# Order of a group's four projections: keys, first queries, values, second queries

## What is computed

```python
proj = x @ w_in                                   # queries, and keys/values of three branches
q_rot = apply_rope(q, cos, sin)                   # rotary position on queries
k_slc = apply_rope(kv_heads(ks), cos, sin);  v_slc = kv_heads(vs)
k_win = apply_rope(kv_heads(kw), cos, sin);  v_win = kv_heads(vw)
s_c = einsum(qn, k_cmp) * scale                   # compressed branch, unrotated queries
s_s = einsum(qr, k_sel) * scale;  s_w = einsum(qr, k_band) * scale
out = g0 * softmax(s_c) @ v_cmp + g1 * softmax(s_s) @ v_sel + g2 * softmax(s_w) @ v_band
```

## Time and profile before

| | us |
|---|---|
| median of 3 runs | 1373.08 (1370.35 to 1373.63) |
| the profiled execution | 1374.31 |
| its span, first to last instruction | 1372.5 |
| scores of the first unit start at | 91.44 |
| last product of the last group starts at | 330.07 |

### The profile page before, as it was taken

The page is one execution under the profiler, slowest core; times in us unless marked ns, Lnnn a source line. Parts: engine busy times, 40 slices in busy tenths (PEclk is TensorE's granted clock), DMA queues, the critical chain, the costliest instruction groups (busy, mean ns, idle before and its releaser), DMA issues.

```text
span 1372.5 us, 19855 instructions
## 1 busy us (share of the span) xinstructions
PE 1322.0 (96%) x6858; PEld 1108.3 (81%) x6858; DVE 635.4 (46%) x1469; ACT 674.6 (49%) x1257; POOL 599.4 (44%) x399
## 2 busy tenths in 40 slices
PE   8979999979999999999999999998999999999997
PEld 6868887867898888888888788887898888888885
DVE  3347777775544433440006767768354343341005
ACT  4347777765444444442214767776354444443122
POOL 2267767763434444444444222222244444444441
PEclk9999999999999999999999999999999999999999
DMA  9442322222323333334333321322424333334321
GB/s 296 108 102 61 85 70 78 69 70 97 99 82 108 92 95 103 92 105 131 101 92 95 87 62 49 94 64 62 154 78 123 92 92 98 100 93 137 103 66 62
DMA packets 172798, 131.98 MB, mean 96 GB/s; under 512 B 24544, under 2 KB 156244, under 8 KB 172724
## 3 DMA queue, kind: packets, MB, share of 16 engines
q1 hardware_dynamic: 172724, 131.02, 33.0%
HBM read 117.17 MB, written 4.39 MB: 89 GB/s over the span
## 4 chain that ended last, share of the span: by engine, by line
PE 82%; DVE 5%; issue 4%; ACT 4%; POOL 2%; DMA 2%; SPq 1%; DVEq 0%; POOLq 0%; ACTq 0%
PE ps L964 15%; PE ps L965 15%; PE ps L966 15%; PE ps L1218 7%; PE ps L1221 7%; PE ps L1219 7%; PE ps L1124 3%; PE ps L1138 2%; PE ps L1091 2%; PE ps L1264 2%; PE ps L1260 2%; PE ps L1259 2%; DVE ptl L1507 1%; DVE prob L1489 1%; PE ps L1137 1%
## 5 line engine op out<-in xcount | busy, mean ns | idle before, releaser
L488 POOL TENSOR_TENSOR wl<-raw,wh 128x1024 fp32r<-128x1024 f32 x178 | 426.3, 2398 | 648.0 <-ACT wh L611 647.9
L964 PE MATMUL ps<-xh,wh 128*128 128x512 f32 x968 | 381.8, 394 | 4.2 <-ACT work L900 3.9
L965 PE MATMUL ps<-xl,wh 128*128 128x512 f32 x968 | 377.9, 390 | 0.0
L966 PE MATMUL ps<-xh,wl 128*128 128x512 f32 x968 | 377.4, 390 | 0.0
L611 ACT ACTIVATE wh<-raw 128x1024 fp32r<-128x1024 f32 x192 | 201.2, 1050 | 191.8 <-PE ps L1221 182.2
L964 PEld LDWEIGHTS ps<-xh,wh 128*128 128x128 f32 x968 | 182.2, 188 | 41.9 <-ACT work L900 5.8
L966 PEld LDWEIGHTS ps<-xh,wl 128*128 128x128 f32 x968 | 181.9, 188 | 38.8
L965 PEld LDWEIGHTS ps<-xl,wh 128*128 128x128 f32 x968 | 182.1, 188 | 33.4
L1664 DVE SCALAR_TENSOR_TENSOR work<-ps,conv,work 128x511 f32<-128x511 f32 x88 | 66.0, 750 | 222.0 <-ACT work L847 156.7
L705 ACT ACTIVATE prob<-prob,negmax 128x128 f32<-128x128 f32 x192 | 107.4, 559 | 69.4 <-DVE negmax L1489 67.5
L1218 PE MATMUL ps<-wh,gh 128*128 128x512 f32 x352 | 137.1, 390 | 0.0
(11 more groups left out here) (197 smaller groups left out, 1948.8 us busy)
## 6 DMA issues: line engine op xcount, KB each, us to landing
raw<-in_ffn_w_up SPq DMA_DIRECT2D x88, 512.0 KB, 3.8
raw<-in_ffn_w_down SPq DMA_DIRECT2D x44, 512.0 KB, 3.6
raw<-in_fox_w_in SPq DMA_DIRECT2D x24, 512.0 KB, 4.0
raw<-in_nsa_w_in SPq DMA_DIRECT2D x12, 512.0 KB, 4.9
xt<-in_x SPq DMA_DIRECT2D x8, 512.0 KB, 5.0
raw<-in_nsa_w_in SPq DMA_DIRECT2D x16, 256.0 KB, 3.8
qs<-work SPq DMA_DIRECT2D x32, 128.0 KB, 2.3
raw<-in_nsa_w_o SPq DMA_DIRECT2D x8, 512.0 KB, 4.1
```

Source lines behind the costliest of these rows:

```text
L488: nc.gpsimd.tensor_tensor(wl[:, slot, :, :], raw[:, slot, :, :], wh[:, slot, :, :].bitcast(F32), ALU.subtract).then_inc(s_wl, 1)
L964: nc.tensor.matmul(o, ah, bh, start=start, stop=False)
L965: nc.tensor.matmul(o, ah, bl, start=False, stop=False)
L966: return nc.tensor.matmul(o, al, bh, start=False, stop=stop)
```

## The change

The order of a group's items becomes keys, queries 0, values, queries 1 (`KIND`). The queries 1 of group g are no longer projected before the group starts but in its own first six steps (`NSA_STEPS`): two ksteps in each of steps 0 and 1, then one in each of steps 2 to 29; steps 30 and 31 have none. So group 0's queries 1 leave the prologue, and the last group has eight ksteps in its steps 0 to 5. `NSA_EARLY` starts in step 8 instead of 2. The work on an item stands two steps earlier in its pass of eight steps (copy in step 5 instead of 7, sine product in 7 instead of 1). The values are transposed in step 30 instead of 19.

```diff
+KIND = (0, 2, 1, 3)
-NSA_EARLY = {2: (0, 0), 6: (1, 0), 12: (2, 0), 18: (3, 0), 21: (0, 1), 24: (1, 1), 27: (2, 1), 30: (3, 1)}
+NSA_EARLY = {8: (0, 0), 11: (1, 0), 14: (2, 0), 17: (3, 0), 20: (0, 1), 23: (1, 1), 26: (2, 1), 29: (3, 1)}
+NSA_STEPS = [(0, 2), (2, 4)] + [(v + 2, min(v + 3, 32)) for v in range(2, 32)]
@@ SP
-            for n in range(6, NSA_ITEMS):
-                item_moves(n - 6)
+            load_item(6)
+            item_moves(1)
+            for n in range(7, NSA_ITEMS):
+                if n > 8:
+                    item_moves(n - 7)
                 load_item(n)
@@ POOL, prologue
-            for n in range(3):
-                if n != 1:
-                    rope_cos(0, n)
-                    rope_sum(0, n)
-                    for h in range(1 if n else 2):
-                        rope_lo(0, n, h)
-                lo(n + 7, (n + 7) % R)
+            for n in range(2):
+                rope_cos(0, n)
+                rope_sum(0, n)
+                for h in range(1 if n else 2):
+                    rope_lo(0, n, h)
+            for c in range(7, 10):
+                lo(c, c % R)
@@ POOL, in the groups
-                    if turned and w == 0:
-                        rope_cos(*item)
-                    if turned and w == 2:
-                        rope_sum(*item)
+                    if 3 < n <= NSA_ITEMS and before[1] != 2:
+                        if w == 0:
+                            rope_sum(*before)
+                    if n < NSA_ITEMS and n % 4 != 2 and w == 6:
+                        rope_cos(*divmod(n, 4))
@@ ACT, in the groups
-                    if g < GROUPS - 1 and w == 7:
-                        item_copy(g + 1, v // 8)
+                    if n < NSA_ITEMS and w == 5:
+                        item_copy(*divmod(n, 4))
@@ DVE, in the groups
-                    if turned and w == (6 if item[1] == 1 else 1):
-                        item_dve(*item)
+                    if n < NSA_ITEMS and n % 4 != 2 and w == 7:
+                        item_dve(*divmod(n, 4))
+                    if v == 0 and g:
+                        item_dve(g, 2)
@@ PE, in the groups
-                    if g < GROUPS - 1:
-                        n = 4 * (g + 1) + v // 8
-                        if v % 8 == 0:
-                            pe.wait_ge(s_pf, n)
-                        kstep(4 + n, (4 + n) % R, v % 8)
+                    for s in range(*NSA_STEPS[v]):
+                        n = 4 * g + 3 + s // KB
+                        if n < NSA_ITEMS:
+                            if s % KB == 0:
+                                pe.wait_ge(s_pf, n)
+                            kstep(4 + n, (4 + n) % R, s % KB)
-                    if v == 19 and g < GROUPS - 1:
-                        pe.wait_ge(s_cl, u // 16 + 1)
-                        values_turn(g + 1)
+                    if v == 30 and g < GROUPS - 1:
+                        pe.wait_ge(s_cmask, u // 16 + 2)
+                        values_turn(g + 1, BX)
```

More of the change, by code:

```diff
@@ L405, in load_out @@
                 for k in range(KB):
[L406 to L408 removed]
+                    if c0 == C_WO0 and k < 7:
+                        item_moves(NSA_ITEMS - 7 + k)
+                    if c0 == C_WO0 and k == 7:
                         move_queries(NSA_ITEMS - 1)
@@ L598, in _ @@
             for g in range(GROUPS):
-                for n in range(2):
+                for n in (0, 2):
                     RAW_EXTRA[(4 + 4 * g + n) % R] += 1
             def landed(c):
-                return sum(2 if 4 <= x < C_WO0 and (x - 4) % 4 < 2 else 1 for x in range(c + 1) if x % R == c % R)
+                return sum(2 if 4 <= x < C_WO0 and x % 2 == 0 else 1 for x in range(c + 1) if x % R == c % R)
             def hi(c, slot, n=None):
@@ L752, in _ @@
                     u, w = 32 * g + v, v % 8
-                    item = (g, 3) if v < 8 else (g + 1, v // 8 - 1)
-                    turned = v < 8 or g < GROUPS - 1
+                    n = u // 8 + 3
                     for x in ([0, 1, 2] if u == 0 else [v + 2]):
@@ L776, in _ @@
                         heads_hi(u // 16 - 1, oh)
[L777 to L781, removed]
+                    if 3 < n <= NSA_ITEMS and n % 4 != 3 and w == (n % 4 == 1):
+                        item_hi(*divmod(n - 1, 4))
+                    if v == 31 and g < GROUPS - 1:
+                        item_hi(g + 1, 2)
+                    if u // 8 < NSA_ITEMS - 2 and w == 2:
+                        hi(u // 8 + 10, (u // 8 + 10) % R)
             head_copy(HEADS - 1, 4 * HEADS, BO + 1)
@@ L1113, in cmp_turn @@
                 pe.wait_ge(s_cp, j + 1)
+                if j % 2 == 0 and j:
+                    pe.wait_ge(s_pl, 2 * j + 3)
                 for i in range(QT):
@@ L1164, in first_tile @@
                 down_half(c0 + k, k, 0, h, oh, ol, OUT_AT, k == 0, False)
+            pe.wait_ge(s_kc, 3)
+            item_steps(0)
+            conv_turn(0)
+            item_steps(1)
+            cmp_hidden(1)
+            pe.wait_ge(s_kc, 4)
+            item_steps(2)
+            pe.wait_ge(s_gel, 2)
+            for g in range(GROUPS):
+                for hb in range(2):
+                    last = nc.tensor.matmul(ps[0:NCMP, 4, g * HD:(g + 1) * HD], ghid[:, hb, g * NCMP:(g + 1) * NCMP], w2v[:, hb, :],
+                                            start=(hb == 0), stop=(hb == 1))
+            last.then_inc(s_cmpo, 1)
             pe.wait_ge(s_cmpr, 1)
             cmp_scores(0)
-            item_steps(3)
+            values_turn(0, BO)
+            conv_turn(1)
             pe.wait_ge(s_vc, 4)
@@ L1571, in _ @@
             conv_copy(1)
-            for step in (cmp_mask, cmp_difference, cmp_sum, cmp_inverse, cmp_gate, cmp_scale):
+            for step in (cmp_sum, cmp_inverse, cmp_gate, cmp_scale):
                 step(0)
```

119 lines of the change are left out of this document (52 added, 67 removed).

## The result

| | kernel before | changed kernel |
|---|---|---|
| median (lowest to highest), us | 1373.10 (1370.35 to 1373.63) | 1382.55 (1381.74 to 1383.22) |
| span of the profiled execution, us | 1372.5 | 1381.0 |
| mean granted clock | 0.994 | 0.988 |

The ratio is 1.0069, with a 95% interval of 1.0053 to 1.0085: **slower by 9.4 us**, where the prediction said 6.7 us faster. The prediction was wrong in its sign, and 1382.55 lies outside its range. (One execution of a later run, at a mean granted clock of 0.842, took 1492.48 us; it is among the ten of that run's median, 1377.22, and is left out of its ratio.)

The account below looks back on a forecast made before the run. PE was taken to bound groups 0 to 2, the chain over DVE, ACT and POOL the last. Prologue -6.3, groups -0.9, last group 0, less 0.5 for lateness: -6.7, 1366.4 us; range 1362.5 to 1371.5.

Parts of the forecast that it names:

- Its first step: Groups 0 to 2: PE, busy 56.8 of 59 us in a filled group, was taken to set the pace.
- Part 1: Prologue: one item leaves and queries 0 come first, so unit 0's maximum comes 6.3 us earlier (bounds 5 and 7.5).
- the rule on the rings: Prologue: rings work in issue order, so scores would wait for two weight loads, some 1 us later than 84.7.
- Part 2: Groups 0 to 2: PE's 58 us each stay; -1.9 us gained and 1.0 us of crowding added, net -0.9 us.
- The gain at the group starts: Starts of groups 1 to 3: PE's waits of 0.6 us for the queries' transfer fall away, -1.9 us.
- The term for crowding: Groups 0 to 2: moved work on ACT, POOL and DVE costs 1.0 us over three groups, bounds 0 and 4.
- Part 3: Last group: the moved item's 5.5 us of PE come back; net taken as 0, range -1.3 to +2.4 us.
- the case I had given -1.3: Last group: swap takes 4 us, DVE waits some 1.5 us, second block takes 14.5 us; -1.3 us, weighed 2 to 1.
- the 0: Last group: net change taken from short and long swap landings weighed 2 to 1, range -1.3 to +2.4 us.
- B: Groups 0 to 2: ACT's backlog in steps 17 and 18 reaches PE, 4 us per group, +6.2, 1379.3 us; chance 0.08.

## Why the prediction was wrong

**Its first step.** "So groups 0 to 2 go at PE's pace" was read from 96% busy and from 56.76 busy of 59.00. The kernel before without swaps shows PE's pace: 171.4 us for units 0 to 96. Before stood 8.0 us above it. The chain over four engines paid part of each wait already (12.8 us of waits, 8.0 us of time), so there was no free cover to lay new waits under. PE's list of waits showed it, in nine short ones that come to 6.2 us: besides the two lines of rows 6 it has this one.

```profile
PE ps L1138 <- DVE ptl L1507: 2.4, 4, 0.8
```

No line of it is long, and I had looked for long ones.

**Part 1** held. -5.7 against -6.3: scores at 85.5 where I had 84.3 to 84.7. The miss lies in the moves: the scores came 3.3 us after the issue of the last one was over, not 2.2:

```profile
79.64 1.33 SPq L365 DMA_DIRECT2D qs<-work  x2
81.02 1.23 SPq L368 DMA_DIRECT2D qs<-work  x2
```

That is the 1 us of the rule on the rings that I had weighed and not taken (the Trainium skill, DMA: Bandwidth & Descriptors, Queues, rings and completion order); the trace agrees with it in size, and in the run with the moves ahead of the loads the last two landed 2.4 us after they were issued, where they took 3.6 here. DVE was done with its list at 85.4, as the 85.6 had it, but then waited 0.83 us for those scores, so its maximum was at 86.23. PE waited 6.0 us, where I had 4.8.

**Part 2** is the failure: +13.4 for -0.9. The gain at the group starts was real, PE's list has no wait there any more. The term for crowding, 1.0 with bounds of 0 and 4, was mis-sized by 14: with the gain of 1.9 it came to 15.3, 5.1 us a group. Even its own bound did not add up, since 0.8 us at two places per group is 4.8 and not 4. It rested on "the nearest row is POOL's wait, 0.8 us per group", which priced a crowd in the order of before and not one more in a place that has no slack. Without swaps that crowding is 9.1 us. And one cost wasn't in the list at all, the waits for the swaps, whose place moved with the sine product from w = 1 to w = 7: they cost 4.4 us more. That the place is the reason is not shown, since a late swap awaited in w = 1 was as dear (15.7 us for 20.2 us of waits).

**Part 3** held in the sum. The moved item's 5.5 us of PE are hidden: 52.3 us against 52.9. DVE had the swap in under 4 us from its issue, so the case I had given -1.3 came, with -0.6; the 0 was the mean of two cases, of which one came. In that case I had too small a wait: DVE waited 2.3 us where I had 1.5, and the second block took 15.4 us for 14.5. The clock stayed at 1.00 behind PE's wait (DVE's row, PE's, and the stretch behind it):

```profile
297.96 0.69 DVE L1485 TENSOR_TENSOR work<-work,sinT 128x512 f32<-128x512 f32 x1 [2.27 <-DMA work<-qf]
```

```profile
299.85 0.38 PE L1124 MATMUL ps<-pth,vv 128*128 128x256 f32 x1 [2.32 <-DVE ptl L1511]
```

```profile
300.00:302.00 2.00, 2.00 (x18) 1.94 (x19) 0.98 (x4) 1.43 (x5) 1.84 (x3) 1.00 0.00 0
```

**The rivals.** B was the one that happened, with its sign in the trace (a wait of over 1 us in steps 17 to 21). Its price was near, 4 us a group for the 5.1 measured; its 1379.3 came as close as it did by luck, since it counts 2.4 us of a late swap in the last group that did not come. It had 0.08, on the argument that "PE's products lie one to three units behind ACT". That is a lead of PE's in the order, not in time. B named ACT's backlog; the runs show that it works through POOL, which stands in its list at what ACT is late with; DVE's waits for the swaps, which B does not have, come on top. The rest, +1.3 behind unit 127, I did not take apart; across the kernels of this study the same stretch took 1045.0 to 1049.7 us.

The new order of the items is not at fault by itself: with the rotation's steps later its time is 0.9939 of the kernel before's. What was not tried is the kernel before with longer swaps; without swaps it took 1361.2, so it may have some of that gain too.

## What to carry to other kernels

Before new work is put under the cover of a "busy" engine, measure that engine's own pace, for instance by leaving out a transfer that others wait for, and add up its short waits; the difference to the present time is about what the waits cost already. When a step is moved within lists that engines work off in order, look at each pair of maker and user on two engines: the user's place must lie behind the maker's by the maker's lateness, or everything queued behind the user is late as well. Give a transfer's waiter more steps before anything else; here two more steps were worth some 16 us.

## What the runs showed of the hardware

DVE and POOL hold each other up. In the prologue DVE's multiplication of two small tiles in SBUF (8 columns, by the gates) took 1.71 us in the changed kernel and ended, at 84.94, with POOL's low part of a weight (82.58 + 2.34); in the version with the moves ahead and DVE's new order it took 1.18 us and again ended at POOL's end, 84.8:

```profile
83.62 1.18 DVE L1554 TENSOR_TENSOR cstat<-cstat,gate 128x8 f32<-128x8 f32 x1
```

```profile
82.40 2.37 POOL L499 TENSOR_TENSOR wl<-raw,wh 128x1024 fp32r<-128x1024 f32 x1 [4.01 <-ACT wh L622]
```

With that low part moved into the groups it took 0.17 us:

```profile
83.82 0.17 DVE L1556 TENSOR_TENSOR cstat<-cstat,gate 128x8 f32<-128x8 f32 x1
```

The reduction and the reciprocal of DVE ran their usual 0.41 and 0.20 us while POOL was at it. The other way round, POOL's cosine product took 1.63 us where it takes 1.28, when it began (68.77) while DVE's sine product ran (68.58 to 69.27):

```profile
68.77 1.63 POOL L517 TENSOR_TENSOR work<-qf,cosT 128x512 f32<-128x512 f32 x1 [0.17 <-POOL kw L541]
```

The Trainium skill (SBUF — State Buffer, Terms) calls it a shared port pair of the two engines, exclusive and held for the full instruction; the traces agree. `cmp_scale` shows it in the groups too: 1.20 us for 0.42 beside POOL's sum, in steps 15 and 16. It is not a new cost of the change, though: the multiplication and `cmp_scale` together took 0.83 + 0.74 us at that place before and 0.17 + 1.20 after. By how much it delays the groups in all, no run here separates.

The granted clock fell to 0.50 behind PE's waits of 2.4 us in step 19 in groups 1 and 2 of the changed kernel. It stayed at 1.00 behind the 2.3 us in the last group and also behind the same wait of 2.4 us in group 0, which ends at 129.19:

```profile
129.00:131.00 2.00, 1.71 (x9) 1.23 (x9) 1.08 (x5) 1.58 (x5) 1.81 (x3) 1.00 0.00 0
131.00:133.00 2.00, 1.89 (x11) 1.67 (x12) 1.63 (x6) 1.60 (x5) 2.00 (x4) 1.00 0.67 152
```

The changed kernel without swaps has a wait of 1.9 us that ends at 125.14 us (group 0), at 186.54 (group 1) and at 246.90 (group 2), and behind the first alone the clock is low:

```profile
127.00:129.00 2.00, 1.94 (x5) 1.60 (x6) 1.09 (x3) 1.29 (x4) 2.00 (x4) 0.50 0.72 154
129.00:131.00 2.00, 2.00 (x12) 1.74 (x11) 1.17 (x5) 1.30 (x3) 2.00 (x3) 0.75 0.33 113
...
188.00:190.00 2.00, 1.79 (x10) 1.33 (x9) 1.64 (x7) 1.43 (x4) 2.00 (x4) 1.00 0.55 113
```

Its block in group 0 is longer by 1.35 us (17.98 us against 16.63), about what the two slow stretches cost. For waits of about 2 us the loss of clock comes on top or doesn't, so an estimate needs both ends.
